# Projecting the prompt queries in the query section's first visit, ahead of the convolution sections, in a hybrid decoder step

## The reference

```python
xn = rmsnorm(hp, norm1)
qa, ka, va, qkv_b, z, b_raw, a_raw = project(xn, w_in, q_norm, k_norm)   # one 1024 x 3592 projection
oa = diff_attn_prompt(qa, ka, va, lam, slopes)           # 4 heads, queries and keys RMS-normed per 64 columns
ob, s_new = gdn_prompt(*gdn_inputs(qkv_b, ...))          # short convolution, gated delta rule, 4 heads
hp = hp + merge_heads(oa, ob, z, ...)                    # output norms, concatenation, output projection
hp = hp + peer_ffn(rmsnorm(hp, norm2), peer_wq, peer_keys, peer_u, peer_v)
```

## Time and profile before

| | us |
|---|---|
| median of 3 runs (2047.03 to 2055.94) | 2050.31 |
| time of the profiled execution | 2046.96 |
| its span | 2045.1 |
| PE busy in the span | 1691.6 (83%) |
| DVE busy | 1335.3 (65%) |
| ACT busy | 802.0 (39%) |
| POOL busy | 785.1 (38%) |
| DMA over the span | 758.91 MB, mean 371 GB/s |

### The profile page before, as it was taken

The page is one execution under the profiler, slowest core; times in us unless marked ns, Lnnn a source line. Parts: engine busy times, 40 slices in busy tenths (PEclk is TensorE's granted clock), DMA queues, the critical chain, the costliest instruction groups (busy, mean ns, idle before and its releaser), DMA issues.

```text
span 2045.1 us, 20559 instructions
## 1 busy us (share of the span) xinstructions
PE 1691.6 (83%) x6211; PEld 853.0 (42%) x6211; DVE 1335.3 (65%) x3023; ACT 802.0 (39%) x2371; POOL 785.1 (38%) x670
## 2 busy tenths in 40 slices
PE   7697999988897878989787888978997657866777
PEld 2242464547453445445344544533563213522111
DVE  1344514344897657897665888775688967679544
ACT  1342322131645523563453346354344423333332
POOL 2111110111444444435444353534444555554442
PEclk9798999999999989999898999999999888987999
DMA  9999823226999999999999999999999999999997
GB/s 333 358 309 382 263 92 118 93 104 244 406 414 409 427 428 428 426 426 411 428 421 429 426 426 400 416 426 393 427 427 426 427 427 427 427 427 427 427 427 313
DMA packets 137015, 758.91 MB, mean 371 GB/s; under 512 B 15263, under 2 KB 24495, under 8 KB 60472
## 3 DMA queue, kind: packets, MB, share of 16 engines
q0 software_dynamic: 88448, 622.22, 73.4%
q1 hardware_dynamic: 44976, 128.07, 16.8%
q10 hardware_dynamic: 3480, 7.31, 1.0%
HBM read 741.56 MB, written 16.26 MB: 371 GB/s over the span
## 4 chain that ended last, share of the span: by engine, by line
PE 38%; DMA 30%; DVE 16%; ACT 7%; issue 4%; SPq 3%; POOL 2%; ACTq 0%; DVEq 0%; POOLq 0%
DMA sb_uv<-in_peer_uv,sb_eidx 27%; PE bank L2224 16%; PE bank L1827 8%; DVE sb_uv L1806 7%; PE bank L2151 3%; PE bank L2191 2%; DVE sb_hres L1780 2%; SPq L841 1%; POOL sb_uv L1006 1%; SPq L845 1%; ACT sb_diag L1384 1%; DMA sb_w<-in_w_sections 1%; PE bank L1941 1%; ACT sb_ew L1377 1%; PE bank L1953 1%
## 5 line engine op out<-in xcount | busy, mean ns | idle before, releaser
L2224 PE MATMUL bank<-sb_uv,sb_diag 128*128 128x512 f32 (+1 forms) x1860 | 943.2, 643 | 277.8 <-ACT sb_diag L1384 267.8
L1006 POOL DMA_INDIRECT sb_uv<-in_peer_uv,sb_eidx x576 | 704.1, 1222 | 829.8 <-PE bank L2224 646.4
L1806 DVE CUSTOM_DVE_ANT_0 sb_uv<-sb_uv,sb_xn 128x1024 f32<-128x1024 f32 x576 | 698.9, 1220 | 280.5 <-DMA sb_uv<-in_peer_uv,sb_eidx 277.6
L2224 PEld LDWEIGHTS bank<-sb_uv,sb_diag 128*128 128x128 f32 (+1 forms) x1860 | 333.8, 194 | 766.4 <-ACT sb_diag L1384 440.7
L1373 ACT ACTIVATE sb_gel<-sb_h 128x1 f32<-128x1 f32 x576 | 116.3, 202 | 753.5 <-DVE sb_h L1806 750.4
L1827 PE MATMUL bank<-sb_w,sb_xnT 128*128 128x512 f32 (+1 forms) x560 | 270.3, 626 | 24.7 <-DMA sb_w<-in_w_sections 11.7
L1384 ACT ACTIVATE sb_diag<-sb_stay,sb_ew 128x128 f32<-128x128 f32 (+1 forms) x465 | 183.2, 394 | 45.7 <-PE bank L2224 2.5
L1377 ACT ACTIVATE sb_ew<-sb_gel,sb_gate 128x1 f32<-128x1 f32 x576 | 169.7, 295 | 19.8
L1827 PEld LDWEIGHTS bank<-sb_w,sb_xnT 128*128 128x128 f32 (+1 forms) x560 | 100.6, 190 | 149.8 <-issue 122.6
L1780 DVE SCALAR_TENSOR_TENSOR sb_hres<-sb_uv,sb_ew,sb_hres 128x1024 f32<-128x1024 f32 x111 | 142.2, 1281 | 0.1
L2191 PEld LDWEIGHTS bank<-sb_rT,sb_zone 128*128 128x128 f32 x832 | 99.3, 193 | 15.7 <-issue 15.3
(11 more groups left out here) (352 smaller groups left out, 1593.2 us busy)
## 6 DMA issues: line engine op xcount, KB each, us to landing
sb_zone<-in_w_route SPq DMA_DIRECT2D x11, 2304.0 KB, 11.8
sb_w<-in_w_sections SPq DMA_DIRECT2D x40, 512.0 KB, 7.3
sb_zone<-in_w_mixer SPq DMA_DIRECT2D x8, 2048.0 KB, 15.6
sb_uv<-in_peer_uv,sb_eidx POOLq DMA_INDIRECT x576, 14.0
sb_sS<-in_cache_kT SPq DMA_DIRECT2D x32, 256.0 KB, 7.3
sb_zone<-in_cache_kT SPq DMA_DIRECT2D x32, 256.0 KB, 7.2
sb_held<-in_cache_v SPq DMA_DIRECT2D x32, 256.0 KB, 7.0
sb_zone<-in_cache_v SPq DMA_DIRECT2D x32, 256.0 KB, 5.9
```

The costliest lines, as they stand in the source:

```text
L1006: nc.gpsimd.indirect_dma_start(uv[:, m % RING, :], None, i["peer_uv"], bass.IndirectOffsetOnAxis(ap=eidx[:, t % 2, n:n + 1], axis=0)).then ...
L1806: nc.vector.tensor_tensor_reduce(out=uv[:, m % RING, 0:D], in0=uv[:, m % RING, 0:D], in1=xn2[:, t % 2, :], scale=1.0, scalar=0.0, op0=ALU. ...
L2224: ins = nc.tensor.matmul(bank[half][0:rows, :], lhsT=G["diag"][:, d % DIAGS, 0:rows], rhs=uv[:, m % RING, D + 512 * half:D + 512 * half + ...
```

## The change

The query section's first visit takes all five tiles, its last visit is dropped, and the last visits are values and keys. So the units are: values of tile 4 (0), keys of tile 4 (1), queries of tile 4 and tiles 0 to 3 (2 to 6), convolution (7 to 21), z (22 to 26), values (27 to 30), keys (31 to 34). The queries of all four prompt tiles are turned early, copied to `qst`, stored to memory (`q_spilled`) and loaded again one tile at a time; before, tile 0's stayed on chip. The planned times follow: loads and squares of x earlier, convolution units 8.7 apart instead of 10.4, the units after them 15 apart instead of 12.1.

```diff
-VISITS = [(4, [PT]), (5, [PT]), (6, [PT])] + [(g, ORDER) for g in range(4)] + [(g, list(range(PT))) for g in range(4, NSEC)]
+VISITS = [(4, [PT]), (5, [PT]), (6, ORDER)] + [(g, ORDER) for g in range(4)] + [(g, list(range(PT))) for g in (4, 5)]
-C0 = 3
+C0 = 2 + NT
-QK = [("k", PT), ("q", PT)] + [("k", t) for t in range(PT)] + [("q", t) for t in range(PT)]
+QK = [("k", PT), ("q", PT)] + [("q", t) for t in range(PT)] + [("k", t) for t in range(PT)]
-SUMMED = (20.5, 60, 66, 72, 77)
+SUMMED = (20.5, 45, 56, 63, 70)
...
-    return 6.9 if n < 4 else 10.4 if n < 15 else 12.1 if n < LATE else 9.0
+    return 6.9 if n < 4 else 7.0 if n < C0 else 8.7 if n < Z0 else 15.0 if n < LATE else 9.0
...
-    n = QK_UNIT[u] + (2 if QK[u][0] == "k" else 1)
-    return after(n, -0.05 if u == NT + 1 else -0.1)
+    return after(QK_UNIT[u] + 1, -0.1)
...
-            if n == C0:
+            if n == 3:
                 entries += [("turn", 0), ("turn", 1)]
-            entries += [("turn", u) for u in range(2, 2 * NT) if n == QK_UNIT[u] + (2 if QK[u][0] == "k" else 1)]
+            entries += [("turn", u) for u in range(2, 2 * NT) if n == QK_UNIT[u] + 1]
...
-                        yield early_at((1.0, 42, 48, 53, 58)[n])
+                        yield early_at((1.0, 33, 38, 43.5, 48)[n])
...
                 def query_load(n):
-                    yield max(att_at(n - 1, 15), turn_at(2 * NT - 1) + 2.5)
-                    sp.wait_ge(s_sc, 2 * NH * n)
-                    sp.wait_ge(s_qst, 16 * (PT - 1))
+                    yield att_at(n - 1, 15) if n else past_at(NPAIR, 9)
+                    if n:
+                        sp.wait_ge(s_sc, 2 * NH * n)
+                    else:
+                        sp.wait_ge(s_ds, 2 * NPAIR)
+                    for spilled in s_qst:
+                        sp.wait_ge(spilled, 32)
...
-                        yield early_at((0, 28.9, 42, 46, 50)[n])
+                        yield early_at((0, 28.9, 34, 40, 45)[n])
...
-                        if u in (2, 3):
-                            act.wait_ge(s_raw[u % 2], 16 * raw_count(4 * NT - 4 + u))
-                        elif u >= 4:
+                        if u in (NT + 1, NT + 2):
+                            act.wait_ge(s_raw[u % 2], 16 * raw_count(4 * NT - 3 - NT + u))
+                        elif u >= 2:
                             act.wait_ge(s_ss8, u - 1)
...
-                    elif t == 0:
-                        act.wait_ge(s_ds, 2 * NPAIR)
-                        parts = [(qt[:, :, :], 0, 128)]
                     else:
-                        if t + 1 == PT:
-                            act.wait_ge(s_qst, 32)
-                        parts = [(F["qst"][:, (t + 1) % 2, :].rearrange("p (h r) -> p h r", h=NH), 0, 128)]
+                        act.wait_ge(s_vecs, 112)
+                        if t >= 2:
+                            act.wait_ge(s_qst[t % 2], 16)
+                        parts = [(F["qst"][:, t % 2, :].rearrange("p (h r) -> p h r", h=NH), 0, 128)]
...
-                    yield early_at((1, 38, 55, 62, 70)[n])
+                    yield early_at((1, 38, 48, 55.5, 62)[n])
```

More of the change, by code:

```diff
@@ L191, in unit_at @@
         return early_at(22 + 6.9 * n)
-    if n < 15:
-        return early_at(55 + 10.4 * (n - 4))
+    if n < C0:
+        return early_at(55 + 7.0 * (n - 4))
+    if n < Z0:
+        return early_at(77 + 8.7 * (n - C0))
     if n < LATE:
-        return early_at(169.4 + 12.1 * (n - 15))
+        return early_at(207.5 + 15.0 * (n - Z0))
     return -77 + 9.0 * (n - LATE)
@@ L393, in hybrid_step @@
         s_kst = [sem(f"k_stored{r}") for r in range(2)]
-        s_qst = sem("q_spilled")
+        s_qst = [sem(f"q_spilled{r}") for r in range(2)]
         s_vst = sem("v_stored")
@@ L527, in entry_bank @@
             return e % 2, e // 2
-        stores = [(s_kst[0], 16 * kst_count(4)), (s_kst[1], 16 * kst_count(5)), (s_vst, 16 * (NT + 1)), (s_cvo, 32), (s_sst, 16 * (NH + 1))]
+        stores = [(s_kst[0], 16 * kst_count(2 * NT - 2)), (s_kst[1], 16 * kst_count(2 * NT - 1)), (s_vst, 16 * (NT + 1)), (s_cvo, 32), (s_sst, 16 * (NH + 1))]
         first_done = [(s_ss, NT), (s_xnT, NT), (s_nrm, 2 * NT), (s_cs, 3 * NT), (s_sst, 16 * NH), (s_snd, 3 * NH), (s_vmeta, 16)] + [(s_spill[m % 3], 16 * spill_count(m)) for m in range(3 * NT - 3, 3 * NT)]
-        second_done = [(s_proj, 4 * len(UNITS)), (s_bank[0], (len(entries) + 1) // 2), (s_bank[1], len(entries) // 2), (s_kst[0], 16 * kst_count(4)), (s_kst[1], 16 * kst_count(5)),
-                       (s_raw[0], 16 * raw_count(4 * NT - 2)), (s_raw[1], 16 * raw_count(4 * NT - 1)), (s_qst, 16 * (PT - 1))]
+        second_done = [(s_proj, 4 * len(UNITS)), (s_bank[0], (len(entries) + 1) // 2), (s_bank[1], len(entries) // 2), (s_kst[0], 16 * kst_count(2 * NT - 2)), (s_kst[1], 16 * kst_count(2 * NT - 1)),
+                       (s_raw[0], 16 * raw_count(4 * NT - 2)), (s_raw[1], 16 * raw_count(4 * NT - 1)), (s_qst[0], 32), (s_qst[1], 32)]
         xn2, score, eidx, best, gate, uv = (G[name] for name in ("xn2", "score", "eidx", "best", "gate", "uv"))
@@ L739, in q_spill @@
                     sp.wait_ge(s_bank[b], k + 1)
-                    sp.dma_start(q_sp[t], F["qst"][:, (t + 1) % 2, :]).then_inc(s_qst, 16)
+                    sp.dma_start(q_sp[t], F["qst"][:, t % 2, :]).then_inc(s_qst[t % 2], 16)
                 def gdn_loads(u):
@@ L872, in _ @@
                 work += [Stream(spills(m)) for m in range(3 * NT) if m % NT] + [Stream(z_store(n)) for n in range(NT)] + [Stream(k_store(u)) for u in range(2 * NT) if QK[u][0] == "k"]
-                work += [Stream(q_spill(t)) for t in range(1, PT)] + [Stream(gdn_loads(u)) for u in range(NT)] + [Stream(query_load(n)) for n in range(1, PT)]
+                work += [Stream(q_spill(t)) for t in range(PT)] + [Stream(gdn_loads(u)) for u in range(NT)] + [Stream(query_load(n)) for n in range(PT)]
                 work += [Stream(resident_loads())] + [Stream(route_loads(n)) for n in range(PT)] + [Stream(residual_load(n)) for n in range(NT)] + [Stream(past_biases())]
@@ L1044, in unit_copy @@
                         else:
-                            act.wait_ge(s_ss8, c + 1)
+                            act.wait_ge(s_ss8, NT + c)
                         if g < 3:
@@ L1152, in conv_silu @@
                         act.wait_ge(s_vecs, 112)
+                        if m < 2:
+                            for spilled in s_qst:
+                                act.wait_ge(spilled, 32)
                         if m >= 2:
@@ L2040, in attention_head @@
                     if h == 0 and n == 0:
-                        for kind, k in (("unit", V0), ("turn", 0), ("turn", 2), ("turn", NT + 1)):
+                        for kind, k in (("unit", V0), ("turn", 0), ("turn", NT + 1)):
                             b, at = entry_bank(kind, k)
                             pe.wait_ge(s_bank[b], at + 1)
-                    if h == 0 and n:
-                        pe.wait_ge(s_qt, 16 * n)
+                    if h == 0:
+                        pe.wait_ge(s_qt, 16 * (n + 1))
                     if h == 0 and n + 1 == PT:
```

## The result

| | before | changed |
|---|---|---|
| median, us (6 runs each) | 2052.97 | 2065.43 |
| span of the profiled execution | 2045.1 | 2063.1 |
| first gather starts | 493.53 | 507.81 |
| from there to the end of the span | 1551.6 | 1555.3 |

The ratio is 1.0063, 95% interval 1.005 to 1.0076: the change makes the kernel slower by 12.5 us. The first gather moved by 14.3 us.

The account below looks back on a forecast made before the run. PE's idle time ahead of the first gather was taken as the bound, one for one. Removing 39.1 us and adding 36.8 gave 2.3 us gained: 2048 on the median's scale, range 2033 to 2061.

Parts of the forecast that it names:

- (f): PE halts near 42 us because unit 3's copy waits for the key stores: 32.0 us added, 29.0 of it idle.
- (a): PE's waits around the first turns and for past keys at the zone's scores go, with clock loss: 10.3 us removed.
- (b): PE's 12.52 us wait at the small columns for early tables goes, plus 3.0 for the clock: 15.5 us removed.
- (c): PE's wait for a weight piece behind the last past keys shrinks from 9.7 to 6.6 us: 3.1 removed.
- (d): PE's waits at the past weights and sums, 2.21 and 1.43 us, get more units around them: 3.6 removed.
- Rival B: Slower, chance 0.14: packed DMA demand makes weight pieces late; one further stall of 12.1 us gives 2060, two 2072.
- (h): Delta rule of tile 4 begins with four units fewer to fill its chain's gaps: 2.4 us added, bounds 0 and 20.
- (e): At the prompt attention's start a 1.06 us wait and slow matmuls go: 4.1 removed; `qkn` copy waits: 2.5 more.
- The low clock: Across the front, PE loses about 3.0 us per low-clock restart; counted as removed at some waits, added at the halt.
- (g): Four prompt query units in a row, each with a turn; PE waits for copies where banks meet: 2.4 us added.

Follow-up runs that it names:

- e1: Changed kernel with the sample tile's two key stores issued ahead of the past keys: ratio 0.9998 to the kernel before, median 2051.5 us.
- e3: Kernel before with the three table loads for the small columns issued ahead of the first past values: ratio 0.9980, median 2048.5 us.
- e4: Changed kernel with every convolution step planned 4 us later: ratio 1.0016 to the kernel before, median 2053.8 us.
- e9: Changed kernel with most past keys and values of the last three pairs not loaded: ratio 1.0025 to the kernel before, median 2054.3 us.
- e7: Changed kernel with units after the convolutions planned 16 us apart instead of 15: ratio 1.0070 to the kernel before, median 2065.8 us.
- e13: Changed kernel with the last two units planned 1.5 us earlier: ratio 1.0083 to the kernel before, median 2067.0 us.
- e14: Changed kernel, halt left in, convolution steps 4 us later and weight piece 23 ahead of the last past values: ratio 1.0005, median 2053.2 us.
- e10: Kernel before with most past keys and values of the last three pairs not loaded: ratio 0.9999, median 2051.2 us.

## Why the prediction was wrong

The forecast was 2048, range 2033 to 2061, the same with 0.55; measured were 2065.4, slower by 0.6%, for which it gave 0.17. Its frame held: gathers start to end unchanged within 4 us (1551.6 and 1555.3), the front bound by PE's idle time one for one (between these two kernels; e1 lost part of it to busy time), the halt. Point by point:

- **(f), the halt, right in place and cause.** Forecast from 42 to 71 us, 29.0; measured from 39.2 to 64.8, 25.6. Both ends came earlier, and the store landed 4.0 us after its issue at 59.81, not in the 7.6 taken from the earlier trace rows. The DMA share was 0.70 then (59 to 64 us), where it was 1.05 at the stores of the kernel before (62 to 71 us); the four later stores of this line, from 418 to 471 us at a share of 0.30, landed in 2.0 in both kernels. The figures of the Trainium skill's page "DMA: Bandwidth & Descriptors", section "Anatomy of one DMA — SWDGE (gpsimd) path", give 2.1 us for the 32 KB of this store, as an estimate. The 4.0 measured lie between that and the loaded row. The error of 3.4 us was to the good.
- **(a), (b), right.** The waits behind the first turns and for past keys, and the 12.5 at the small columns, are gone. e3 shows that this wait was worth 4 us and not 15.5 in the kernel before, as the next one took over. In the changed kernel the halt lies in front of it and takes it in, and e1 measures the two together: of the 24.6 us of halt that it takes off, 9.7 go to the wait for the tables, 6.0 in its profile to PE's busy time, and 13.3 are gained by the ratios (8.3 by the start of the gathers in the profile).
- **(c), right.** 6.6 forecast, 7.1 measured.
- **(d), the step that failed first.** "have more units standing around them: 3.6 less". They were 5.4 us in all (4.0 at the past weights, 1.4 at the sums) and are 9.1 now (1.9 and 7.2). I counted units of PE as cover, and didn't look at what stands ahead of the copies on ACT and DVE. The planned distance of the convolution units went from 10.4 to 8.7 while PE needs some 12 for one, with the past's work between them (from 95.83 to 219.06 for ten); so, as I read it, convolution steps stand too early in the written order for when their rows can be there, and where their rows are late they hold up a copy that has nothing to do with them. e4 moves just these steps and gets 9.6 us back. No run changed the spacing alone, so that it was the 8.7 that put them there is not shown. Rival B had the packed transfers, and e9 shows their part (7.8 us), but it looked for the stall at weight pieces and gave it 0.14.
- **(h) and (e), too small.** In the chains of the delta rule 2.4 were added; measured are 6.1 more (3.2 for `kb` became 6.2 for `kqT`, 1.2 for `hres` 2.9, and 1.4 at the last product is new). The start of the attention, counted as 1.1 less, is 3.4 more. The waits for `qkn` (2.5) went as forecast. Of the `kqT` part e4 shows that it is again convolution steps ahead of a copy. That the 4.5 is missing cover was my reading; e7 and e13 put quarters around and ahead of it and gained nothing. What sets the length of that last chain is open.
- **The low clock, not gained.** I took off 3.4 + 3.0 + 3.0 us for restarts that fell away, and added 3.0, net 6.4. PE's busy time came out the same (433.9, 433.8). Behind the halt sixteen recorded matmuls took 8.97 us where 7.07 is normal, 1.9 lost and not 3.0. The granted clock was 0.67 between 34 and 75 us and 0.85 between 196 and 242 now, where it was 0.64 between 75 and 94 before; the restarts went elsewhere.

The sum for the first gather's start: 7.3 us from (d), 4.5 from (e), 3.7 from (h), 6.4 from the clock, 0.5 from (c), less 3.4 at (f) and 0.6 at (g) (1.8 measured in short waits for 2.4), is 18.4. The start came at 507.8 and not at 491.2, 16.6 later; the terms come to 1.8 more than that, which is open. In time the forecast was 2.3 faster and the result 12.5 slower, a miss of 14.8. e4 gives 9.6 of it back by the place of the convolution steps alone; in its trace 6.4 of the wait at the past sums go, a part of (d), and 3.2 of the one for `kqT`, a part of (h). e14's 11.9 has the wait for the weight piece in it too, and that one the forecast had counted in (c), so it is no part of the miss.

## What to carry to other kernels

When a step is moved in a written order, ask of every engine what now stands directly ahead of the copies that the critical engine waits for; a step that waits for late data there can cost most of its wait (PE waited 7.16 us behind a step of ACT that waited 9.69), whatever units the critical engine was given as cover. When one buffer is reused earlier, look for its last reader's place in the queues, a store's too: here one line's place on SP was worth some 13 us. A wait ahead of another wait is not worth its length: the 25.6 us halt was worth 13.3, the 12.5 us wait 4, since each covered or was followed by another. And count the busy time of the critical engine beside its idle time: in e1 6.0 of the 14.3 us of idle time that went came back as busy time of the same matmuls.

## What the runs showed of the hardware

With 24 MB of transfers less the kernel before did not get faster (0.9999), though the DMA share of its front fell from 1.02 to 0.46 between 142 and 192 us: a share near 1 did not mean that bytes were what it waited for there. A store of the keys landed in 8.6 us at a share of 1.05 and in 4.0 at 0.70 (32 KB both), and a larger one (256 KB) in 2.0 at 0.30.

Up to the first gather PE was busy from 431.4 to 439.8 us over the sixteen profiled kernels, each time with the same 1890 recorded instructions; it was most in e1, which had less idle time than the changed kernel and a lower granted clock (0.87 against 1.00 between 75 and 142 us). What engine activity led to that clock is not settled by these runs. The gathers took 1549.6 to 1558.0 us from their start to the end of the span over the sixteen profiled kernels, without a pattern in the orders tried, so one profile of each can't settle differences of the whole span under some 8 us. e10 and the kernel before have the same instructions and bytes for their first 78 us, and yet PE came to the small columns' first matmul at 88.76 in one and 87.43 in the other.
